# A twelfth ring slot for expert pieces, filled during the second mixer

## The chip, the cores and the metric

The kernel runs on one core of a Trainium2 chip. The metric is the device time of one execution in microseconds (us). The kernel before took 689.34 us, the median of three runs (689.18 to 690.75).

## The reference

One call computes two transformer blocks on 256 tokens of width 1024, all in float32.

- The first block is a mixer (a gated convolution and a gated linear attention in both directions) and a gated MLP of inner width 2816 with a convolution.
- The second block is a mixer (latent attention with 8 heads and an mLSTM with 4 heads, joined and multiplied by `w_o`), then a mixture of experts, then a gated embedding path ("PLE"), and a final norm.

The part that matters here is the mixture of experts and what follows:

```python
g_top, g_idx = lax.top_k(softmax(hf @ w_rg + b_rg), 1)               # 1 of 4 groups
e_top, e_idx = lax.top_k(softmax(e_in), TOP_K)                       # 2 of its 8 experts
# for each token and chosen expert e:
y = (silu(x @ w_g[e]) * (x @ w_u[e])) @ w_d[e]                       # 1024 -> 256 -> 1024
x = x + weighted sum of y
x = x + (p @ w_ple) * sigmoid(rmsnorm(x) @ w_ple_gate)
return rmsnorm(x, final_norm_g)
```

There are 32 experts with three matrices of 1024 x 256 each. Which experts a token takes is known only when the router has run, but with 256 tokens every expert's weights are loaded: 32 x 3 MB, about 100 MB of the 175 MB that the kernel moves.

## The kernel before

The program is written out by hand for each engine: a block of instructions for SP (SyncE, which issues nearly all loads), GpSimd, ScalarE, VectorE and TensorE. Each engine runs its own list in order, and semaphores tie the lists together. `sig(name)` is a semaphore; several steps that follow one another can share one (`STEPS`), and `at(name, n)` is the count at which step `name` has been done n times.

**Expert pieces.** The host lays the expert weights out as `w_moe`: 8 groups of 4 experts, each group cut into 6 pieces of 128 x 4096 floats (2048 KB): four for the gate and up matrices (a quarter of the 1024 rows each) and two for the down matrix. So there are 48 pieces. They come in through a ring of slots. Three more loads go through the same ring: `w_ple` (item 42, 1024 KB, put between pieces 41 and 42) and the two halves of `w_ple_gate` (the last two items, 49 and 50). An *item* is a place in that order of 51; up to item 41 item n is piece n, and items 43 to 48 are pieces 42 to 47.

**The ring.** The kernel before has 11 homes for items (`HOMES`, L339 to L343), each 4096 floats wide on all partitions: six slots of the tile `W` (which holds weight panels in the earlier stages), four stretches of the tile `arena` (work space of the earlier stages) and `hh` (the normed and the transposed tokens). Item n goes to home n mod 11. The homes come free at different times of the second mixer, so SP's list fills them one after the other as their last readers finish (L521 to L542): item 0 into `W` slot 2 once the query weights are used, parts of items 1, 2 and 4 piecemeal as attention gets on, item 3, then items 5 to 10. The last of these, item 10, goes into `hh` when the router's logits are done. From item 11 on (L545 to L559) SP waits until the piece that was 11 items before it has been used in the last round of its group, and then issues the load.

**The expert stage.** TensorE goes through the 8 groups in order. A group takes one or more rounds of 32 token slots for each of its 4 experts; here there are 9 rounds in all, two of them in the second group. A round is: gather the tokens (L2302), multiply them with the four up pieces (L2318), scatter the results of the round before (L2324), turn the activations, and multiply with the two down pieces (L2378). Ahead of each piece TensorE waits for its landing (`landed_chunk`, L2290). Ahead of the last group stands `ple_product` (L2402), which multiplies by `w_ple`. Five filler matmuls (L2374) stand ahead of the wait for the last down piece. Behind the last group come the last scatter, the transposes, and the product with `w_ple_gate`, whose weights are split on ScalarE (L1014) and VectorE (L1730) into a rounded part and a rest (`wpg_high`, `wpg_low`), as are the tokens (`hpT`).

**The mixer's weights.** At the end of the first block SP issues two panels of `w_in_2` (L500, L501), the query and key/value weights (L502, L503) and three small ones (L504 to L506). Then it waits for the first projection (`a2_used`) and issues one half of `w_o` (L508); then for the z product (`zw_used`) and issues the other half (L510). ScalarE rounds `w_o` in pieces between its other work (L893).

Of the kernel before, what the change touches and what calls it, by code (L numbers as in the profile page):

```python
# [22 lines left out]
P = 128  # L23
# [3 lines left out]
KD = D // P  # L27
# [27 lines left out]
CPG = UPC + DNC  # L55
NCHUNK = NGRP8 * CPG
UNIT = 4096
SLOTS = 6
RING = SLOTS + 5
PLE_AT = 42  # L60
# [9 lines left out]
def build(nc, a, out):  # L70
    with ExitStack() as ctx:
# [10 lines left out]
                        ("mq_done", 2), ("sa_done", 6), ("mk_done", 2), ("mv_done", 2), ("nt_done", 1)),  # L82
            "pe_route": (("oT_done", 2), ("hmT_done", 2), ("pT_done", 1), ("y2_done", 2), ("logits_done", 2), ("rank_done", 1)),
            "act_mix1": (("lr_ready", 1), ("q_ready", 1), ("ln_ready", 1), ("k_ready", 1), ("v_ready", 2),
# [11 lines left out]
                         ("max_ready", 12), ("nmax_ready", 1), ("nm_ready", 1)),  # L96
            "dve_route": (("hmn_ready", 8), ("ym_ready", 2), ("gsub_ready", 1), ("sel_ready", 1), ("msub_ready", 1)),
        }
# [28 lines left out]
        W_at = -(-nc.sbuf_base // 32) * 32  # L127
        W = sb("W", [P, SLOTS * UNIT])
        junk_at = -(-nc.sbuf_base // 32) * 32
        junk = sb("junk", [P, D])  # L130
# [207 lines left out]

        HOMES = [W[:, s * UNIT:(s + 1) * UNIT] for s in (2, 3)]  # L339
        HOMES += [arena[:, FRONT + s * UNIT:FRONT + (s + 1) * UNIT] for s in range(3)]  # L340
# [5 lines left out]
        def ring(n):  # L346

            return HOMES[n % RING]

        def item(chunk):  # L350
# [8 lines left out]
        pw = v3(ring(PW_ITEM)[:, 0:2048], 2)  # L359
        sgate = v3(ring(PLE_AT + 2)[:, 0:2048], 2)  # L360
        assert ring(PLE_AT + 1) is HOMES[RING - 1]

# [45 lines left out]
        wpg = [ring(NCHUNK + 1 + h).rearrange("p (k n) -> p k n", k=KD) for h in range(2)]  # L408
        assert (NCHUNK + 1) % RING == 5 and (NCHUNK + 2) % RING == 6
# [32 lines left out]
        def _(sp):  # L442
# [62 lines left out]
            sp.dma_start(wm[:, 1], a["w_mk_2"][0].rearrange("h d e -> d h e")).then_inc(sig("wm_landed"), 16)  # L505
            sp.dma_start(wm[:, 2], a["w_mv_2"][0].rearrange("h d e -> d h e")).then_inc(sig("wm_landed"), 16)  # L506
            sp.wait_ge(sig("a2_used"), 1)
# [5 lines left out]
            def load_chunk(n):  # L513
                g, j = divmod(chunk_of(n), CPG)
                sp.dma_start(ring(n), w_moe[g, j]).then_inc(sig(f"ring{n % RING}_landed"), 16)

# [10 lines left out]
            load_part(4, 0, 1800)  # L527
            sp.wait_ge(sig("sel_built"), 8)
            load_part(1, 3008, UNIT)
            sp.wait_ge(sig("st_done"), 6)  # L530
            load_part(1, 1536, 3008)
            load_part(2, 0, 2048)
            sp.wait_ge(sig("num_done"), 4)
            load_part(4, 1800, UNIT)
            sp.wait_ge(sig("pv_done"), 4)
            load_part(2, 2048, 3088)
# [147 lines left out]
        def _(act):  # L684
# [323 lines left out]
            def round_gate(pieces):  # L1008

                for n in pieces:  # L1010
                    h, q = divmod(n, 4)
                    m = NCHUNK + 1 + h
                    act.wait_ge(sig(f"ring{m % RING}_landed"), 16 * (m // RING + 1))
                    act.copy(wpg_high[h][:, 2 * q:2 * q + 2, :], wpg[h][:, 2 * q:2 * q + 2, :]).then_inc(sig("dense_high"), 1)  # L1014
# [63 lines left out]
        def _(dve):  # L1078
# [621 lines left out]
            for g in range(NGRP8):  # L1700
                if g == NGRP8 - 1:
                    for q in range(4):
                        b, half = divmod(q, 2)
                        dve.wait_ge(sig("pw_done"), q + 1)
# [41 lines left out]
            lower_gate((6, 7))  # L1746
            dve.wait_ge(sig("pw_ready"), 4)
            dve.wait_ge(sig("xs_ready"), 4)
# [19 lines left out]
        def _(pe):  # L1768
# [622 lines left out]
            def ple_product(done):  # L2391

                pe.wait_ge(sig("pT_ready"), at("pT_ready", 1))
                landed_chunk(PLE_AT)
                pe.wait_ge(sig("sc_ready"), done + 1)
                pe.wait_ge(sig("xgb_ready"), done + 1)
                for q in range(4):
                    b, half = divmod(q, 2)
                    if q >= 2:
                        pe.wait_ge(sig("pw_ready"), q - 1)  # L2400
# [4 lines left out]
                pe.wait_ge(sig("pw_ready"), 4)  # L2405

# [79 lines left out]
```

## Time and profile before

| | |
|---|---|
| median of three runs | 689.34 us |
| lowest, highest | 689.18, 690.75 us |
| span of the profiled execution | 686.0 us |
| time of the profiled execution beside its span | not recorded apart; the three runs above lie 3.2 to 4.8 us over the span |
| TensorE matmul, weight load | 636.9 us, 481.4 us |
| VectorE, ScalarE, GpSimd | 379.4, 277.6, 56.3 us |
| bytes moved | 174.75 MB, mean 255 GB/s |

How to read the rows further down. A row of the timeline has the start and the length of a piece of work in us, its engine, its line in the kernel, the operation, what it writes and reads, how many instructions were merged (x16), and in brackets how long the engine had been idle before and what ended that. SPq is SP's queue: its rows are the issues of loads, not their duration; a long one means that SP was held while issuing. A row of the stretches has the busy time of each engine with its count of instructions, then the clock granted to TensorE (1.00 is full), the mean busy share of the 16 DMA engines, and what they moved in GB/s. A row of the chain has a start, a length, and what the chain passed through. A row of the page's DMA issues has the size of each and the median time from issue to landing.

### The profile page before, as it was taken

Reading aid. Unit: us, or ns where it says so; the run is one execution under the profiler, and the core shown is the slowest. Engines: PE = TensorE matmul, PEld = TensorE weight load, DVE = VectorE, ACT = ScalarE, POOL = GpSimd, SP = SyncE. Lnnn points to the kernel's source line nnn. Section 1 sums busy time; section 2 is a strip of 40 time slices with the busy share of each in tenths; the row PEclk is TensorE's granted clock in tenths of the full one; section 3 lists DMA queues with packets and bytes.
Section 4 is the critical chain, followed back from the end, with each engine's and each line's share of the span. In section 5 each row is a group of like instructions: output and inputs, shape, how many; then the busy total and the mean of one; then the engine's idle time right before and its main releaser. Section 6 shows DMA issues by size and latency. Waiting matters only on the chain.

```text
span 686.0 us, 11096 instructions
## 1 busy us (share of the span) xinstructions
PE 636.9 (93%) x4347; PEld 481.4 (70%) x4347; DVE 379.4 (55%) x666; ACT 277.6 (40%) x431; POOL 56.3 (8%) x81
## 2 busy tenths in 40 slices
PE   7999999999999999999999999999999866768895
PEld 4999997799999999996697788744444332324364
DVE  6686965668766677767768465542222220203195
ACT  6764373556555555545755721311111000000193
POOL 1000000400000000003084610000000000000010
PEclk9999999999999999999999999999999998989998
DMA  8944541757755555204903548999899999999931
GB/s 324 349 144 148 199 147 33 262 159 244 234 187 187 188 187 188 97 0 140 330 38 122 188 182 308 364 425 427 362 431 426 428 427 428 427 425 428 408 140 61
DMA packets 55209, 174.75 MB, mean 255 GB/s; under 512 B 4743, under 2 KB 29443, under 8 KB 48899
## 3 DMA queue, kind: packets, MB, share of 16 engines
q1 hardware_dynamic: 54496, 172.54, 65.9%
q10 hardware_dynamic: 674, 1.69, 0.7%
q8 instruction: 26, 0.43, 0.3%
q14 instruction: 13, 0.10, 0.0%
HBM read 173.17 MB, written 1.05 MB: 254 GB/s over the span
## 4 chain that ended last, share of the span: by engine, by line
PE 68%; DMA 19%; DVE 7%; ACT 3%; issue 2%; another core or an unknown queue 0%; POOLq 0%; POOL 0%; DVEq 0%; ACTq 0%
PE ps L1801 15%; PE ps L1803 15%; PE ps L1802 15%; DMA arena<-in_w_moe_dram 14%; PE ps L2318 5%; DMA W<-in_w_moe_dram 4%; PE ps L2302 2%; PE ps L2378 2%; PE ps L1998 2%; PE ps L2324 1%; PE ps L2425 1%; PE ps L2146 1%; DVE arena L1458 1%; PE ps L2097 1%; PE ps L2161 1%
## 5 line engine op out<-in xcount | busy, mean ns | idle before, releaser
L1801 PE MATMUL ps<-hT_high,w_up_parts 128*128 128x256 f32 x352 | 99.8, 283 | 0.0
L1803 PE MATMUL ps<-hT_high,w_up_parts 128*128 128x256 f32 x352 | 99.6, 283 | 0.0
L1802 PE MATMUL ps<-hT_low,w_up_parts 128*128 128x256 f32 x352 | 99.6, 283 | 0.0
L1801 PEld LDWEIGHTS ps<-hT_high,w_up_parts 128*128 128x128 f32 x352 | 67.5, 192 | 0.5
L1802 PEld LDWEIGHTS ps<-hT_low,w_up_parts 128*128 128x128 f32 x352 | 67.5, 192 | 0.4
L1803 PEld LDWEIGHTS ps<-hT_high,w_up_parts 128*128 128x128 f32 x352 | 67.5, 192 | 0.0
L1289 DVE TENSOR_TENSOR w_up_parts<-W,w_up_parts 128x1024 fp32r<-128x1024 f32 x44 | 52.8, 1227 | 25.5 <-ACT w_up_parts L818 25.5
L818 ACT CAST w_up_parts<-W 128x1024 fp32r<-128x1024 f32 x44 | 44.7, 1047 | 29.7 <-PE ps L1803 29.7
L988 ACT ACTIVATE sg<-ps 128x256 f32<-128x256 f32 x9 | 3.5, 384 | 122.3 <-PE ps L2318 122.3
L1801 PE MATMUL ps<-h_high,dense_high 128*128 128x256 f32 x160 | 45.7, 286 | 0.0
L2318 PE MATMUL ps<-W,junk 128*32 128x512 f32 x304 | 37.2, 618 | 9.0 <-DMA W<-in_w_moe_dram 9.0
L1802 PE MATMUL ps<-h_low,dense_high 128*128 128x256 f32 x160 | 45.3, 283 | 0.0
L1803 PE MATMUL ps<-h_high,dense_low 128*128 128x256 f32 x160 | 45.3, 283 | 0.0
L1314 DVE SCALAR_TENSOR_TENSOR arena<-ps,arena 128x255 f32<-128x255 f32 x80 | 33.1, 477 | 17.5 <-ACT arena L838 17.1
L2302 PEld LDWEIGHTS ps<-arena,x_tok 128*128 128x128 f32 x288 | 32.9, 192 | 11.2 <-issue 11.2
L1172 DVE TENSOR_TENSOR dense_low<-W,dense_high 128x1024 fp32r<-128x1024 f32 x32 | 37.2, 1221 | 1.9 <-ACT dense_high L755 1.9
L2302 PE MATMUL ps<-arena,x_tok 128*128 128x128 f32 x288 | 34.5, 278 | 3.2 <-DVE arena L1654 2.0
L755 ACT CAST dense_high<-W 128x1024 fp32r<-128x1024 f32 x32 | 31.3, 1045 | 11.9 <-PE ps L1803 10.0
L1660 DVE TENSOR_TENSOR slots_low<-ps,slots_high 128x512 fp32r<-128x512 f32 x20 | 12.9, 686 | 35.6 <-ACT slots_high L992 35.3
L1801 PE MATMUL ps<-w_down_high,uact_high 128*128 128x512 f32 x80 | 31.3, 392 | 0.5 <-DVE uact_low L1325 0.5
L1681 DVE SCALAR_TENSOR_TENSOR sg<-sg,stat,ps 128x256 f32<-128x256 f32 x9 | 4.3, 480 | 49.3 <-ACT sg L988 49.3
L1801 PEld LDWEIGHTS ps<-h_high,dense_high 128*128 128x128 f32 x160 | 30.7, 192 | 1.1 <-issue 1.1
(480 smaller groups left out, 1355.4 us busy)
## 6 DMA issues: line engine op xcount, KB each, us to landing
W<-in_w_moe_dram SPq DMA_DIRECT2D x24, 2048.0 KB, 22.8
arena<-in_w_moe_dram SPq DMA_DIRECT2D x17, 2048.0 KB, 29.9
W<-in_w_up_dram SPq DMA_DIRECT2D x22, 1024.0 KB, 8.8
W<-in_w_in_dram SPq DMA_DIRECT2D x8, 2048.0 KB, 10.8
W<-in_w_down_dram SPq DMA_DIRECT2D x11, 1024.0 KB, 5.0
hh<-in_w_moe_dram SPq DMA_DIRECT2D x4, 2048.0 KB, 30.2
W<-in_w_out_dram SPq DMA_DIRECT2D x2, 2048.0 KB, 9.0
W<-in_w_o_dram SPq DMA_DIRECT2D x2, 2048.0 KB, 8.3
```

The source lines that it names most:

```text
L755: act.copy(piece(panel_hl(n)[0], n, c), piece(panel(n), n, c)).then_inc(sig("dense_high"), 1)
L818: act.copy(w_up_hl[0][:, c], U[q][:, :, g, i * P:(i + 1) * P]).then_inc(sig("up_high"), 1)
L1172: dve.tensor_tensor(piece(panel_hl(n)[1], n, c), piece(panel(n), n, c), piece(panel_hl(n)[0], n, c).bitcast(F32), ALU.subtract).then_inc(s ...
L1289: dve.tensor_tensor(w_up_hl[1][:, c], U[q][:, :, g, i * P:(i + 1) * P], w_up_hl[0][:, c].bitcast(F32), ALU.subtract).then_inc(sig("up_low" ...
L1314: dve.scalar_tensor_tensor(o, s, w, o, ALU.mult, ALU.add).then_inc(sig("tap_done"), 1)
L1801: pe.matmul(o, lhs[0], rhs[0], start=first, stop=False, skip_group_check=True)
L1802: pe.matmul(o, lhs[0], rhs[1], start=False, stop=False, skip_group_check=True)
L1803: return pe.matmul(o, lhs[1], rhs[0], start=False, stop=last_k, skip_group_check=True)
L1998: last = pe.matmul(ps[:, 2 + b, 0:424], hT[:, k, b * P:(b + 1) * P], wA[:, k, :], start=(k == 0), stop=(k == KD - 1))
L2302: last = pe.matmul(ps[:, h, (k % 4) * P:(k % 4 + 1) * P], x_tok[:, b, k * P:(k + 1) * P], hot[:, b, :], start=(b == 0), stop=(b == 1))
L2318: last = pe.matmul(ps[CAP * c:CAP * c + CAP, 2, :], xg[:, k, CAP * c:CAP * c + CAP], up_chunk(CPG * g + j)[:, c, kk, :], start=(k == 0), s ...
L2378: last = pe.matmul(ps[CAP * c:CAP * c + CAP, bank, :], aT[:, f, CAP * c:CAP * c + CAP], down_chunk(CPG * g + UPC + f)[:, c, 512 * half:512 ...
```

## The change

There are twelve homes. The new one is a tile of its own, `spare` (128 x 4096 floats), placed behind `W`; the room comes from the reserve for dynamic transfers, which the program now sets to 256 bytes. `spare` is home 0, and the other homes keep their order, each one place further on. SP issues item 0 into it right behind the three small mixer weights, ahead of both halves of `w_o`; each of the waits in the mixer that used to guard item n now guards item n + 1. From item 12 on a reload waits for the piece 12 items before it.

With another count of homes the last items fall elsewhere: the halves of `w_ple_gate` land in `W` slots 2 and 3 (before: `W` slot 0 and the last stretch of the arena), `hpT` moves from `W` slot 3 to slot 1, and `pw` and `sgate` (results of the PLE path) keep to homes whose last piece has been used. The semaphores of `pw_done` and `pw_ready` are given up for places on shared ones, which makes room for that of the twelfth home. The instructions on the compute engines are otherwise the same.

```diff
-RING = SLOTS + 5
+RING = SLOTS + 6
@@ STEPS
             "pe_route": (("oT_done", 2), ("hmT_done", 2), ("pT_done", 1), ("y2_done", 2), ("logits_done", 2), ("rank_done", 1),
+                         ("pw_done", 4)),
-            "dve_route": (("hmn_ready", 8), ("ym_ready", 2), ("gsub_ready", 1), ("sel_ready", 1), ("msub_ready", 1)),
+            "dve_route": (("hmn_ready", 8), ("ym_ready", 2), ("gsub_ready", 1), ("sel_ready", 1), ("msub_ready", 1),
+                          ("pw_ready", 4)),
@@
         W = sb("W", [P, SLOTS * UNIT])
+        spare = sb("spare", [P, UNIT])
@@
-        HOMES = [W[:, s * UNIT:(s + 1) * UNIT] for s in (2, 3)]
+        HOMES = [spare[:]] + [W[:, s * UNIT:(s + 1) * UNIT] for s in (2, 3)]
@@
+        def landings(n):
+            return 16 * (n // RING + 1) + (0, 0, 32, 32, 0, 16, 0, 0, 0, 0, 0, 0)[n % RING]
@@
-        sgate = v3(ring(PLE_AT + 2)[:, 0:2048], 2)
+        sgate = v3(ring(PLE_AT - 1)[:, 0:2048], 2)
@@
-        hpT = [v3(rounded(f"hpT_{part}", W_at, 3 * UNIT + n * UNIT // 2, UNIT // 2), KD) for n, part in enumerate(("high", "low"))]
+        hpT = [v3(rounded(f"hpT_{part}", W_at, UNIT + n * UNIT // 2, UNIT // 2), KD) for n, part in enumerate(("high", "low"))]
@@ SP
             sp.dma_start(wm[:, 2], a["w_mv_2"][0].rearrange("h d e -> d h e")).then_inc(sig("wm_landed"), 16)
+            ...
+            load_chunk(0)
             sp.wait_ge(sig("a2_used"), 1)
             sp.dma_start(PAN[5], w_o[:, :, 512:1024]).then_inc(sig("wo1_landed"), 16)
             sp.wait_ge(sig("zw_used"), 1)
             sp.dma_start(PAN[4], w_o[:, :, 0:512]).then_inc(sig("wo0_landed"), 16)
@@
             sp.wait_ge(sig("uq_used"), 1)
-            load_chunk(0)
+            load_chunk(1)
             sp.wait_ge(sig("mv_done"), at("mv_done", 2))
-            load_part(1, 0, 1536)
-            load_part(2, 3088, UNIT)
+            load_part(2, 0, 1536)
+            load_part(3, 3088, UNIT)
             ...
             sp.wait_ge(sig("y1_high"), 5)
-            load_chunk(3)
+            load_chunk(4)
             for n, (name, count) in enumerate((("half_used", 1), ("ym_ready", at("ym_ready", 2)), ("wo_used", 1), ("wo_used", 1),
-                                               ("wo_used", 1), ("logits_done", at("logits_done", 2))), 5):
+                                               ("wo_used", 1), ("logits_done", at("logits_done", 2))), 6):
                 sp.wait_ge(sig(name), count)
                 load_chunk(n)
@@ TensorE
             def landed_chunk(n):
-                pe.wait_ge(sig(f"ring{n % RING}_landed"), 16 * (n // RING + 1) + (0, 32, 32, 0, 16, 0, 0, 0, 0, 0, 0)[n % RING])
+                pe.wait_ge(sig(f"ring{n % RING}_landed"), landings(n))
@@
-    nc = _bacc.Bacc("TRN2", target_bir_lowering=False, num_devices=1)
+    nc = _bacc.Bacc("TRN2", target_bir_lowering=False, num_devices=1, dynamic_dma_scratch_size=256)
```

## Rows read from the trace of the kernel before

**Rows 1.** Page, busy time and DMA queues.
```profile
PE 636.9 (93%) x4347; PEld 481.4 (70%) x4347; DVE 379.4 (55%) x666; ACT 277.6 (40%) x431; POOL 56.3 (8%) x81
...
q1 hardware_dynamic: 54496, 172.54, 65.9%
```

**Rows 2.** Stretches: busy us by engine, clock, DMA share, GB/s.
```profile
346.00:378.00 32.00, 31.30 (x205) 26.85 (x204) 24.34 (x39) 16.73 (x26) 22.48 (x10) 1.00 0.19 66
...
442.00:486.00 44.00, 42.31 (x324) 21.11 (x324) 17.64 (x57) 7.54 (x13) 0.00 (x0) 1.00 1.01 428
...
486.00:492.00 6.00, 6.00 (x55) 2.35 (x58) 1.71 (x4) 0.00 (x0) 0.00 (x0) 1.00 0.67 224
...
492.00:650.00 158.00, 129.71 (x927) 56.52 (x919) 34.21 (x67) 12.41 (x28) 0.00 (x0) 0.95 1.01 426
```

**Rows 3.** Chain of waits, expert stage: start, length, what.
```profile
546.08 49.73 DMA arena<-in_w_moe_dram
...
602.66 44.64 DMA arena<-in_w_moe_dram
```

**Rows 4.** TensorE's timeline, expert stage.
```profile
546.69 1.93 PE L2318 MATMUL ps<-W,junk 128*32 128x512 f32 x16 [1.99 <-DMA W<-in_w_moe_dram]
...
595.85 1.92 PE L2318 MATMUL ps<-arena,junk 128*32 128x512 f32 x16 [0.82 <-DMA arena<-in_w_moe_dram]
...
600.74 1.92 PE L2318 MATMUL ps<-W,junk 128*32 128x512 f32 x16 [2.60 <-DMA W<-in_w_moe_dram]
...
618.24 8.04 PE L2402 MATMUL ps<-W,arena 128*128 128x512 f32 x16 [0.34 <-DMA W<-in_w_ple_dram]
...
642.53 1.92 PE L2378 MATMUL ps<-arena,sg 128*32 128x512 f32 x16 [0.47 <-DMA arena<-in_w_moe_dram]
...
647.34 1.92 PE L2378 MATMUL ps<-arena,sg 128*32 128x512 f32 x16 [1.52 <-DMA arena<-in_w_moe_dram]
```

**Rows 5.** SP's queue, second mixer.
```profile
326.62 5.10 SPq L506 DMA_DIRECT2D W<-in_w_mv_dram  x1
...
337.39 0.37 SPq L508 DMA_DIRECT2D W<-in_w_o_dram  x1
...
378.74 0.34 SPq L515 DMA_DIRECT2D W<-in_w_moe_dram  x1
```

**Rows 6.** SP's queue, beginning of the expert stage.
```profile
436.97 1.28 SPq L515 DMA_DIRECT2D W<-in_w_moe_dram  x3
...
465.96 0.33 SPq L515 DMA_DIRECT2D W<-in_w_moe_dram  x1
...
488.90 0.33 SPq L515 DMA_DIRECT2D arena<-in_w_moe_dram  x1
```

**Rows 7.** Stretches in the second mixer.
```profile
337.00:338.00 1.00, 0.70 (x5) 0.46 (x4) 1.00 (x3) 0.26 (x1) 0.00 (x0) 1.00 0.10 27
...
342.00:344.00 2.00, 2.00 (x19) 2.00 (x19) 1.90 (x10) 1.97 (x3) 0.00 (x0) 1.00 1.04 396
```

**Rows 8.** Page, DMA issues by tile: count, size, us to landing.
```profile
W<-in_w_in_dram SPq DMA_DIRECT2D x8, 2048.0 KB, 10.8
...
W<-in_w_o_dram SPq DMA_DIRECT2D x2, 2048.0 KB, 8.3
```

**Rows 9.** ScalarE's timeline, second mixer.
```profile
351.73 1.99 ACT L893 CAST wo_high<-W 128x1024 fp32r<-128x1024 f32 x2
...
357.31 0.60 ACT L917 ACTIVATE arena<-ps 128x512 f32<-128x512 f32 x1 [2.29 <-PE ps L1803]
```

**Rows 10.** ScalarE's timeline, tail.
```profile
652.79 3.90 ACT L1014 CAST wpg_high<-W 128x1024 fp32r<-128x1024 f32 x4
```

**Rows 11.** TensorE's timeline, a piece behind a wait.
```profile
576.04 3.45 PE L2318 MATMUL ps<-W,junk 128*32 128x512 f32 x16 [2.37 <-DMA W<-in_w_moe_dram]
```

**Rows 12.** Stretches with the granted clock, the same place and the tail.
```profile
576.00:579.40 3.40, 3.36 (x16) 0.59 (x16) 0.00 (x0) 0.00 (x0) 0.00 (x0) 0.53 1.01 429
...
647.30:661.00 13.70, 12.11 (x54) 6.18 (x55) 10.01 (x13) 9.43 (x14) 0.00 (x0) 1.00 0.80 298
```

More of the change, by code:

```diff
@@ L82, in build @@
                         ("mq_done", 2), ("sa_done", 6), ("mk_done", 2), ("mv_done", 2), ("nt_done", 1)),
-            "pe_route": (("oT_done", 2), ("hmT_done", 2), ("pT_done", 1), ("y2_done", 2), ("logits_done", 2), ("rank_done", 1)),
+            "pe_route": (("oT_done", 2), ("hmT_done", 2), ("pT_done", 1), ("y2_done", 2), ("logits_done", 2), ("rank_done", 1),
+                         ("pw_done", 4)),
             "act_mix1": (("lr_ready", 1), ("q_ready", 1), ("ln_ready", 1), ("k_ready", 1), ("v_ready", 2),
@@ L359, in build @@
         pw = v3(ring(PW_ITEM)[:, 0:2048], 2)
-        sgate = v3(ring(PLE_AT + 2)[:, 0:2048], 2)
-        assert ring(PLE_AT + 1) is HOMES[RING - 1]
+        sgate = v3(ring(PLE_AT - 1)[:, 0:2048], 2)
+        assert ring(NCHUNK) is HOMES[0] and ring(NCHUNK - 1) is HOMES[RING - 1]
         def up_chunk(n):
@@ L408, in build @@
         wpg = [ring(NCHUNK + 1 + h).rearrange("p (k n) -> p k n", k=KD) for h in range(2)]
-        assert (NCHUNK + 1) % RING == 5 and (NCHUNK + 2) % RING == 6
+        assert (NCHUNK + 1) % RING == 1 and (NCHUNK + 2) % RING == 2
         wpg_low = [rounded("wpg_low0", arena_at, FRONT, UNIT), rounded("wpg_low1", arena_at, FRONT + 3 * UNIT, UNIT)]
@@ L506, in _, with load_chunk @@
             sp.dma_start(wm[:, 2], a["w_mv_2"][0].rearrange("h d e -> d h e")).then_inc(sig("wm_landed"), 16)
+            def load_chunk(n):
+                g, j = divmod(chunk_of(n), CPG)
+                sp.dma_start(ring(n), w_moe[g, j]).then_inc(sig(f"ring{n % RING}_landed"), 16)
+            load_chunk(0)
             sp.wait_ge(sig("a2_used"), 1)
@@ L510, in _ @@
             sp.dma_start(PAN[4], w_o[:, :, 0:512]).then_inc(sig("wo0_landed"), 16)
-            def load_chunk(n):
-                g, j = divmod(chunk_of(n), CPG)
-                sp.dma_start(ring(n), w_moe[g, j]).then_inc(sig(f"ring{n % RING}_landed"), 16)
             def load_part(n, lo, hi):
@@ L521, in _ @@
             sp.wait_ge(sig("uq_used"), 1)
-            load_chunk(0)
+            load_chunk(1)
             sp.wait_ge(sig("mv_done"), at("mv_done", 2))
-            load_part(1, 0, 1536)
-            load_part(2, 3088, UNIT)
+            load_part(2, 0, 1536)
+            load_part(3, 3088, UNIT)
             sp.wait_ge(sig("conv2_done"), at("conv2_done", 4))
-            load_part(4, 0, 1800)
+            load_part(5, 0, 1800)
             sp.wait_ge(sig("sel_built"), 8)
-            load_part(1, 3008, UNIT)
+            load_part(2, 3008, UNIT)
             sp.wait_ge(sig("st_done"), 6)
-            load_part(1, 1536, 3008)
-            load_part(2, 0, 2048)
+            load_part(2, 1536, 3008)
+            load_part(3, 0, 2048)
             sp.wait_ge(sig("num_done"), 4)
-            load_part(4, 1800, UNIT)
+            load_part(5, 1800, UNIT)
             sp.wait_ge(sig("pv_done"), 4)
-            load_part(2, 2048, 3088)
+            load_part(3, 2048, 3088)
             sp.wait_ge(sig("y1_high"), 5)
-            load_chunk(3)
+            load_chunk(4)
             for n, (name, count) in enumerate((("half_used", 1), ("ym_ready", at("ym_ready", 2)), ("wo_used", 1), ("wo_used", 1),
-                                               ("wo_used", 1), ("logits_done", at("logits_done", 2))), 5):
+                                               ("wo_used", 1), ("logits_done", at("logits_done", 2))), 6):
                 sp.wait_ge(sig(name), count)
@@ L1012, in round_gate @@
                     m = NCHUNK + 1 + h
-                    act.wait_ge(sig(f"ring{m % RING}_landed"), 16 * (m // RING + 1))
+                    act.wait_ge(sig(f"ring{m % RING}_landed"), landings(m))
                     act.copy(wpg_high[h][:, 2 * q:2 * q + 2, :], wpg[h][:, 2 * q:2 * q + 2, :]).then_inc(sig("dense_high"), 1)
@@ L1703, in _ @@
                         b, half = divmod(q, 2)
-                        dve.wait_ge(sig("pw_done"), q + 1)
+                        dve.wait_ge(sig("pw_done"), at("pw_done", q + 1))
                         dve.tensor_copy(pw[:, b, 512 * half:512 * half + 512], ps[:, q % 2, :]).then_inc(sig("pw_ready"), 1)
@@ L1746, in _ @@
             lower_gate((6, 7))
-            dve.wait_ge(sig("pw_ready"), 4)
+            dve.wait_ge(sig("pw_ready"), at("pw_ready", 4))
             dve.wait_ge(sig("xs_ready"), 4)
@@ L2399, in ple_product @@
                     if q >= 2:
-                        pe.wait_ge(sig("pw_ready"), q - 1)
+                        pe.wait_ge(sig("pw_ready"), at("pw_ready", q - 1))
                     for k in range(2):
@@ L2404, in ple_product @@
                     last.then_inc(sig("pw_done"), 1)
-                pe.wait_ge(sig("pw_ready"), 4)
+                pe.wait_ge(sig("pw_ready"), at("pw_ready", 4))
             begun = 0
```

## The prediction

> **What bounds the kernel now.** I read the busy shares first, then the busy time by stretches, then the chain that ended last, and last TensorE's and SP's own timelines around the places that matter. The busy shares [rows 1] mislead: TensorE looks like the bound with 93%, and the main DMA queue fills two thirds of the 16 engines. The stretches take them apart [rows 2]. From 442 to 650 us, nearly the whole expert stage, the DMA engines are busy 1.01 of the time at 426 to 428 GB/s, except from 486 to 492 us, where the share is 0.67. From 492 to 650 us TensorE is busy 129.7 of 158 us. In the second mixer, by contrast, the DMA engines have room: their share is 0.19 from 346 to 378 us.
>
> The chain says the same [rows 3]: from 546 to 647 us it is two long DMA steps of expert pieces (49.7 and 44.6 us, each from the issue of a piece to its landing, with others ahead of it in the queue) and a few us of matmuls between them. Behind 647.3 us comes a tail of TensorE, ScalarE and VectorE work. TensorE's timeline shows what one piece costs [rows 4]: it waits for the landings of pieces 37 and 38, at 595.85 and 600.74 us, which are 4.89 us apart, and at the end for those of pieces 46 and 47, at 642.53 and 647.34 us. Piece 47 is the last one, and what follows takes 686.0 - 647.3 = 38.7 us.
>
> So the end is the landing of the last expert piece plus 38.7 us, and that landing is set by how many bytes are still to come when the DMA engines begin to be full at about 442 us.
>
> **The change part by part.**
>
> *One piece leaves the full stretch.* Item 0 now goes into a slot of its own and is issued right behind the three small mixer weights, near 331.7 us instead of at 378.74 [rows 5]. Every other home keeps its trigger: the home that took item n behind a given wait now takes item n + 1 behind the same wait. A reload of item n waits for the release of item n - 12, and that is what item n - 1 waited for before. So at each trigger in the program the loads are exactly one item further on. The place to test this is the one where the queue runs dry for want of a free slot [rows 6]: four items are issued from 437 to 442 us and six more, the first group's releases, up to 465.96; the next issue is at 488.90, when the second round of the second group has used its first piece. Ten transfers of 4.9 us last until about 487 us, hence the share of 0.67. After the change the same number of transfers stands between the same triggers: the gap stays, no longer and no shorter, and behind it 33 items are left instead of 34. Removed: one transfer of 2048 KB, 2.097 MB. By the rates of the full stretch (428 and 426 GB/s) it is 4.90 to 4.92 us; by two landings 4.89. I take -4.9 us.
>
> A rule may be weighed here. The rows show 426 to 428 GB/s. The Trainium skill, page "DMA: Bandwidth & Descriptors", section "Bandwidth", says that for loads from HBM the HBM side binds, at about 358 GB/s for a core; by it a piece is worth 5.9 us and the sum would be 683.5 us. The trace disagrees with it in this kernel, and the sum goes by the trace.
>
> *Does TensorE follow by the whole 4.9 us?* It waits for a piece at 546.69, nearly 2 us, the first such wait [rows 4]; up to there it keeps its times. From there to 650 us it is idle mostly ahead of landings. Where it has less slack than 4.9 us, only the next wait shrinks: it is ready for piece 37 at 595.03, with the landing now at 591.0, so it gains 0.8 us there; it is ready for piece 38 at about 597.3 and finds it landed; piece 39 lands one distance later, at 600.7 in place of 605.6, and there it waits again, the whole 4.9 us earlier. From there on what matters hangs on a landing or on a chain that began with one. The narrowest such chain goes from the landing of w_ple (618.24) over its product and the last group's gather and up products to 642.06, 0.47 us before piece 46 lands; ahead of piece 47 there are another 1.52 us of waiting. I take the whole 4.9; the lower end, if this chain ran 2 to 2.5 us longer, is 4.4.
>
> *What is put in front of the output weights.* Item 0 stands in SP's queue ahead of the second half of w_o, whose issue waits for the first projection until 337.39 us [rows 5]. SP is free from 326.62 + 5.10 = 331.72 us, and the issue of item 0 costs between 0.34 us (L515 at 378.74, into an idle queue) and 5.10 us (L506, the longest issue near it); SP is back at 336.8 at the latest, before the wait ends. Cost in SP's queue: 0. In the DMA engines: the weights ahead have drained by about 337 us (27 GB/s from 337 to 338), [rows 7], then w_o's half takes 8.3 us from issue to landing, to 345.7 us [rows 8]. With 2.1 MB ahead of it at 396 GB/s, 5.3 us, it lands at 351.0 us at the latest, and at 349 if item 0 begins at 336 already. Its first reader is ScalarE at 351.73 us [rows 9], and behind this reader ScalarE has another 2.29 us of idle, until TensorE's z product lets it go on. GpSimd takes the rounded half later still. Cost 0; upper end, if the landing slipped by the length of one more transfer to 356, 2 us.
>
> *The tail's homes.* The gate weights land in W slots 2 and 3 instead of W slot 0 and the arena. Their rounded copies go to W slots 4 and 5, which now hold up pieces of the last group, read before the down product at 642.53; the first rounding starts at 652.79 [rows 10]. hpT's halves go to W slot 1, an up piece of that group as well. hh holds the last group's first down piece, read until 644.45, and is written behind the last scatter. All these writes stand behind the last scatter by their own waits, so this cover doesn't depend on luck. Same number and shapes of instructions: 0, and no reason for a gain.
>
> *Semaphores and scratch.* pw_done and pw_ready move to shared counters whose earlier steps are complete by then; no wait is added: 0. The reserve for dynamic transfers goes from its default to 256 bytes. 172.54 of the kernel's 174.75 MB go over queue q1, named hardware_dynamic, issued by SP [rows 1]; GpSimd issues nothing. I take 0. No row bounds it from above but rival D; from below nothing can be gained.
>
> **Sum.** -4.9 us. The profiled span goes from 686.0 to 681.1 us. The profiled execution has no time of its own beside its span; the three runs lie 3.2 to 4.8 us above it and their median 3.3, which I keep: 689.34 - 4.9 = **684.4 us**. The runs' spread (689.18 to 690.75) puts it between 684.3 and 685.9, the lower end of the gain at 684.9.
>
> **Rivals.**
>
> *A. The clock takes part of it back.* Where TensorE has waited for a piece, its clock can fall: behind a wait of 2.37 us the 16 matmuls of a piece take 3.45 us, at a granted clock of 0.53, which is nearly all at the lower of its two levels (1.2 and 2.4 GHz); the same 16 take 1.92 us at 1.00 [rows 4, 11, 12]. None of this falls into the tail now: the granted clock is 1.00 from 647.3 to 661 us [rows 12]. With every wait moved, it could fall on the last down product, where nothing hides it: 1.5 us, so 685.9 us. Against it: the waits move together, their lengths hardly change, and the five filler matmuls still stand ahead of the last piece. The Trainium skill, page "TensorE: Matmul & The Clock Gate", section "Part 1: The HAM clock gate", tells that a pause in TensorE's activity brings the lower clock back; the rows agree, and it speaks against a change that makes TensorE wait more. Chance 0.08.
>
> *B. The room was not the limit.* If the ring is full by waiting for TensorE anyway, a piece loaded earlier only lengthens the gap at 486 to 492 us, or opens another: gain 0, 689.3 us. For it: the gap itself. Against it: a share of 0.67 in six us and of 1.01 everywhere behind. Chance 0.04.
>
> *C. w_o comes late: slower than before.* Item 0 holds up the second half of w_o, in SP's issue and in the queue. ScalarE's rounding at 351.73 stands in order ahead of the z gate and the mixer's conv activations. It costs from a landing after 351.73 + 2.29 = 354.0 us on, and outweighs the gain from 358.9. With the slowest reading of the rows (SP held once more by 5.1 us behind 337.4, then the 10.8 us from issue to landing that panels of w_in took [rows 8]) I get 353.3, still no cost. To be slower by 0.3%, over 691.4, it takes a landing at 361 us. Chance 0.03, about 692 us.
>
> *D. The smaller scratch slows the transfers.* 0.1 us on each of some 50 loads cancels the gain, 0.2 us on each gives 694 us. The queue's name speaks against it. Chance 0.03.
>
> **How the numbers follow.** Forecast 0.82 (684.4 us), A 0.08 (685.9), B 0.04 (689.3), C 0.03, D 0.03. A measurement of this kernel tells about 0.3%, 2.07 us, from no change, so faster means below 687.3 us: 0.82 + 0.08 = 0.90. Within 0.3%: 0.04 of B and 0.01 of C and D where they stay small, 0.05. Slower: the other 0.05 of C and D. The range holds the forecast's spread (to 685.9), 0.8 us below it for a faster set of runs or the page's rate, and A on top of a slower set: 683.6 to 687.0 us.
>
> **What would show it right or wrong.** Right: an issue of a 2048 KB expert piece near 332 us and full DMA engines until w_o's half has landed, before 351; ScalarE's reader still near 351.7; the first steps of the expert stage and the gap at 486 to 492 us at their present times; the waits for landings 4.9 us earlier by 600 us; the last down product at 642.4; a tail of 38.7 us. Wrong: that product at 642.4 but a longer tail (A); a longer gap (B); the expert stage beginning later (C); less than 426 GB/s in the full stretch (D).

## The result, and the profile after

The changed kernel took 683.26 us, the median of four runs (682.7 to 684.9), against 689.43 us of before (four runs, 689.18 to 690.75): ratio 0.9907 with a 95% interval of 0.9895 to 0.9920. Forecast were 684.4 us and a range from 683.6 to 687.0. The direction was right, and the time lies 1.1 us under the forecast and 0.3 us under the range. Three more comparisons, on three different chips (which chip the first one ran on is not on record), gave smaller gains:

| comparison | before | changed kernel | ratio | interval |
|---|---|---|---|---|
| first | 689.43 | 683.26 | 0.9907 | 0.9895 to 0.9920 |
| second | 690.10 | 685.45 | 0.9930 | 0.9917 to 0.9944 |
| third | 689.66 | 685.90 | 0.9944 | 0.9930 to 0.9957 |
| fourth | 689.97 | 684.91 | 0.9937 | 0.9914 to 0.9959 |

One run of before in the fourth comparison took 2198.93 us and is left out. The mean of the four ratios is 0.9930, a gain of 4.9 us. The intervals of the first and the third comparison do not meet (0.9920 and 0.9930): an interval from one set of runs does not cover what changes from one set to the next. So there are two things to explain: the 4.9 us, and why one comparison of a few runs can give 6.2 and another 3.8.

The span of the profiled execution after is 680.7 us. The stretches that answer to [rows 2 and 7] (busy us by engine, granted clock, DMA share, GB/s):

```profile
337.00:342.00 5.00, 5.00 (x43) 5.00 (x44) 3.85 (x9) 4.49 (x12) 0.00 (x0) 1.00 0.94 390
342.00:346.00 4.00, 4.00 (x36) 4.00 (x35) 1.82 (x11) 3.96 (x7) 1.01 (x1) 1.00 1.05 387
346.00:348.00 2.00, 2.00 (x19) 2.00 (x19) 0.00 (x0) 0.27 (x1) 1.92 (x2) 1.00 0.33 120
...
442.00:486.00 44.00, 42.31 (x328) 21.35 (x326) 17.62 (x56) 7.54 (x13) 0.00 (x0) 1.00 1.00 427
486.00:492.00 6.00, 6.00 (x57) 1.87 (x59) 1.45 (x3) 0.00 (x0) 0.00 (x0) 1.00 0.65 229
492.00:645.00 153.00, 130.02 (x924) 58.26 (x913) 34.54 (x67) 12.73 (x28) 0.00 (x0) 0.94 1.01 425
```

The reader is to see three things. From 337 to 346 us the DMA engines are now busy (0.94 and 1.05; they were at 0.10 from 337 to 338, [rows 7]) and the queue is empty at about 347. The gap at 486 to 492 us is where it was and as large, 0.65 against 0.67 [rows 2]. And the full stretch behind it, cut 5 us earlier at 645 us, still has a share of 1.01, at 425 GB/s: by share and rate it moved 153 us x 425 = 65.0 MB where before moved 158 us x 426 = 67.3 MB, about one transfer of 2.1 MB less.

SP's queue, with the new issue (L517 at 330.95), answers to [rows 5 and 6]; the last line is the first store of the output:

```profile
325.60 5.31 SPq L513 DMA_DIRECT2D W<-in_w_mv_dram  x1
330.95 0.51 SPq L517 DMA_DIRECT2D spare<-in_w_moe_dram  x1
336.68 0.37 SPq L521 DMA_DIRECT2D W<-in_w_o_dram  x1
...
436.22 1.28 SPq L517 DMA_DIRECT2D W<-in_w_moe_dram  x3
...
459.19 6.36 SPq L517 DMA_DIRECT2D arena<-in_w_moe_dram  x3
488.16 0.33 SPq L517 DMA_DIRECT2D W<-in_w_moe_dram  x1
...
672.20 6.17 SPq L573 DMA_DIRECT2D out_dram<-hh  x4
```

SP was held for 0.51 us by the new issue, and issued w_o's half at 336.68 as soon as its wait ended. The whole second block begins 0.71 us earlier than before (first panel at 317.31, was 318.02), and so does all of this: w_o's reader on ScalarE starts at 351.03 us (was 351.73, [rows 9]), the three loads at 436.22 (was 436.97), the first release of the second group at 488.16 (was 488.90). From the block's first panel to the three loads it is 118.91 us, and was 118.95. So the piece ahead of w_o cost the mixer nothing.

TensorE's timeline in the expert stage, with the waits for landings ([rows 4]):

```profile
590.52 1.92 PE L2326 MATMUL ps<-W,junk 128*32 128x512 f32 x16 [0.86 <-DMA W<-in_w_moe_dram]
...
595.42 3.33 PE L2326 MATMUL ps<-W,junk 128*32 128x512 f32 x16 [2.61 <-DMA W<-in_w_moe_dram]
...
600.32 1.92 PE L2326 MATMUL ps<-arena,junk 128*32 128x512 f32 x16 [1.56 <-DMA arena<-in_w_moe_dram]
...
612.94 7.11 PE L2410 MATMUL ps<-W,arena 128*128 128x512 f32 x16 [0.88 <-DMA W<-in_w_ple_dram]
...
637.38 1.92 PE L2386 MATMUL ps<-hh,sg 128*32 128x512 f32 x16
...
642.01 1.92 PE L2386 MATMUL ps<-spare,sg 128*32 128x512 f32 x16 [1.35 <-DMA spare<-in_w_moe_dram]
```

One row of before that stands nowhere yet is that of piece 39:

```profile
605.64 2.88 PE L2318 MATMUL ps<-arena,junk 128*32 128x512 f32 x16 [2.97 <-DMA arena<-in_w_moe_dram]
```

Piece 39 lands at 600.32 (was 605.64) and piece 47 at 642.01 (was 647.34): 5.32 and 5.33 us earlier, of which 0.75 were there before the three loads at 436.22 were issued. Behind piece 47 there are 680.7 - 642.0 = 38.7 us, the same tail as before. One more row of the chain shows the same bound as [rows 3]:

```profile
597.91 44.06 DMA spare<-in_w_moe_dram
```

### The profile page after: what moved, and what is told of

It reads as the page before. It is cut to its first block, busy times and chain, and to the rows that moved or that the text cites. A ratio compares the mean times of both kernels' runs of the same rounds, so it can differ in the third digit from the quotient of the medians.

```text
span 680.7 us, 11095 instructions
## 1 busy us (share of the span) xinstructions
PE 637.0 (94%) x4347; PEld 482.7 (71%) x4347; DVE 379.1 (56%) x666; ACT 277.7 (41%) x431; POOL 56.1 (8%) x81
## 3 DMA queue, kind: packets, MB, share of 16 engines
HBM read 173.17 MB, written 1.05 MB: 256 GB/s over the span
## 4 chain that ended last, share of the span: by engine, by line
PE 73%; DMA 14%; DVE 7%; ACT 2%; issue 2%; another core or an unknown queue 0%; POOL 0%; POOLq 0%; DVEq 0%; ACTq 0%
PE ps L1809 15%; PE ps L1811 15%; PE ps L1810 15%; DMA W<-in_w_moe_dram 7%; DMA spare<-in_w_moe_dram 6%; PE ps L2326 6%; PE ps L2310 3%; PE ps L2386 3%; PE ps L2332 2%; PE ps L2006 2%; PE ps L1781 1%; PE ps L2433 1%; PE ps L2154 1%; DVE arena L1466 1%; PE ps L2105 1%
## 5 line engine op out<-in xcount | busy, mean ns | idle before, releaser
L2326 PE MATMUL ps<-W,junk 128*32 128x512 f32 x368 | 46.2, 630 | 7.5 <-DMA W<-in_w_moe_dram 7.5
L2310 PEld LDWEIGHTS ps<-arena,x_tok 128*128 128x128 f32 x288 | 35.1, 203 | 11.2 <-issue 11.2
L2310 PE MATMUL ps<-arena,x_tok 128*128 128x128 f32 x288 | 36.7, 289 | 3.2 <-DVE arena L1662 2.0
L2326 PEld LDWEIGHTS ps<-W,junk 128*32 128x32 f32 x368 | 10.8, 113 | 31.1 <-issue 20.9
L1810 PE MATMUL ps<-w_down_low,uact_high 128*128 128x512 f32 x80 | 31.3, 391 | 0.0
```

What stands on the lines that cost most here:

```text
L1810: pe.matmul(o, lhs[0], rhs[1], start=False, stop=False, skip_group_check=True)
L2310: last = pe.matmul(ps[:, h, (k % 4) * P:(k % 4 + 1) * P], x_tok[:, b, k * P:(k + 1) * P], hot[:, b, :], start=(b == 0), stop=(b == 1))
L2326: last = pe.matmul(ps[CAP * c:CAP * c + CAP, 2, :], xg[:, k, CAP * c:CAP * c + CAP], up_chunk(CPG * g + j)[:, c, kk, :], start=(k == 0), s ...
```

## The experiments

Two measures serve below. The first is the time of the runs. The second is taken from each profile: from the issue of the three loads at the start of the full stretch (near 437 us) to the first store of the output. It leaves out all that happens in the first block and the mixer. I call it the expert span:

| kernel | expert span, us |
|---|---|
| before | 677.53 - 436.97 = 240.56 |
| reserve alone; tile alone | 240.62; 240.70 |
| changed kernel, four profiles | 235.98, 235.77, 235.68, 235.80 |

By it the ring of twelve gives 240.63 - 235.81 = 4.8 us, and no two profiles of one kind are more than 0.3 us apart. For the pair of profiles shown above it is 240.56 - 235.98 = 4.6 us.

**The reserve alone.** The kernel before with one edit:

```diff
-    nc = _bacc.Bacc("TRN2", target_bir_lowering=False, num_devices=1)
+    nc = _bacc.Bacc("TRN2", target_bir_lowering=False, num_devices=1, dynamic_dma_scratch_size=256)
```

> The kernel before with one edit: the reserve for dynamic transfers is 256 bytes; ring of eleven, all else as before. The changed kernel was 6.2 us faster by the medians where one transfer is worth 4.9; its four runs lie 1.9 to 2.1 us above their spans, where the profiled span of before (686.0) lies 3.2 to 4.8 us below the runs of before. Theory S (the smaller reserve shortens what lies around the span): time 688.0 to 688.4, that is 1.1 to 1.4 us below before, with time minus span near 2.0 here and near 3.3 in before. Rival N (what lies around the span doesn't depend on the reserve, and the extra 1.3 us are the luck of the runs): 689.0 to 689.9, time minus span the same as in the runs of before. Rival D of the prediction (a smaller reserve slows the transfers): slower than before, and less than 426 GB/s in the full stretch.

Measured: 689.98 us against 690.10, ratio 0.9997 (0.9988 to 1.0006), expert span 240.62 us. Theory S fell, and with it rival D of the prediction. Its reason fell too: time minus span is 1.8 to 2.1 us in all runs of this kernel and 1.7 to 2.1 us in those of before beside it. My "3.3 us above the span" had set the span of one run against the median of others.

**The room alone.** The tile is allocated and not used, so all behind `W` stands 16 KB further on; reserve 256 bytes.

```diff
         W = sb("W", [P, SLOTS * UNIT])
+        spare = sb("spare", [P, UNIT])
```

> The kernel before with the tile of the twelfth slot allocated behind W and never used (so junk, gbc, the constants and the arena stand 16 KB further on, as in the changed kernel) and the reserve at 256 bytes; ring of eleven. Theory T: addresses cost and give nothing, ratio 0.999 to 1.001, about the time of before. Rival X by addresses: up to 1.3 us faster, 0.998.

Measured: 689.94 us against 689.66, ratio 1.0000 (0.9991 to 1.0009), expert span 240.70 us. Addresses give nothing beyond the interval, 0.6 us either way.

**Item 0 late.** The changed kernel, with this:

```diff
-            load_chunk(0)
             sp.wait_ge(sig("a2_used"), 1)
...
                 sp.wait_ge(sig(name), count)
+                if n == 8:
+                    load_chunk(0)
                 load_chunk(n)
```

> The changed kernel with item 0 issued not ahead of w_o but between items 7 and 8, at the first wait that lets three loads go (near 436 us); twelve slots as in the changed kernel. Theory F (a transfer is worth its 4.9 us only if it is made while the DMA engines have room; from 437 us on they are full): the item stands in the full stretch again, so the gain over before is only what it fills of the gap at 486 to 492 us (a share of 0.67 in 6 us, 2.0 us): 2.0 us for the ring, plus whatever the reserve gives, so 2.6 to 3.3 us slower than the changed kernel, about 686.2, and the gap gone from the stretches. Rival R (twelve slots are worth it wherever item 0 is issued): like the changed kernel, 683.3. Rival B of the prediction would have the gap as long as before.

Measured: 687.20 us, ratio 0.9961 (0.9947 to 0.9975), against 685.45 us of the changed kernel in the same set. Stretches and queue:

```profile
486.00:492.00 6.00, 6.00 (x57) 2.18 (x60) 1.48 (x4) 0.00 (x0) 0.00 (x0) 1.00 0.99 423
492.00:648.00 156.00, 129.34 (x927) 57.25 (x919) 34.15 (x66) 12.27 (x28) 0.00 (x0) 0.95 1.01 425
```

```profile
436.83 0.33 SPq L517 DMA_DIRECT2D spare<-in_w_moe_dram  x1
437.20 1.46 SPq L517 DMA_DIRECT2D W<-in_w_moe_dram  x3
...
488.68 0.33 SPq L517 DMA_DIRECT2D W<-in_w_moe_dram  x1
```

The gap is gone: a share of 0.99 where it was 0.67, with eleven transfers instead of ten between the same triggers. The expert span, 675.67 - 436.83 = 238.84 us, is 1.8 us shorter than before's, close to the 2.0 us of idle in the gap, and 3.0 us longer than the changed kernel's. By the medians it is 1.75 us slower than the changed kernel (the intervals, to 0.9944 and from 0.9947, just fail to meet), less than the 2.6 to 3.3 expected; by the expert span the 3.0 us are as expected. So a twelfth slot is worth 1.8 us if it is filled when the DMA engines are full already, and 4.8 us if it is filled while they have room. Rivals R and B fell.

**Item 0 with item 1.**

```diff
-            load_chunk(0)
             sp.wait_ge(sig("a2_used"), 1)
...
             sp.wait_ge(sig("uq_used"), 1)
+            load_chunk(0)
             load_chunk(1)
```

> The changed kernel with item 0 issued right ahead of item 1, behind both halves of w_o (near 378 us in place of 331). The DMA engines have room there too: a share of 0.25 from 375 to 380 us and 0.10 from 385 to 390. Theory F: the same as the changed kernel within 0.5 us, since any place with room will do and item 0 ahead of w_o costs nothing. Rival W (item 0 ahead of w_o delays the mixer a little): faster than the changed kernel by up to 1 us. Rival L (items 2 and 3, issued from 389 us, come later for it and so on up to the full stretch): slower by up to 1 us.

Measured: 685.31 us, ratio 0.9934 (0.9920 to 0.9947), beside 685.45 of the changed kernel; expert span 673.01 - 437.01 = 236.00. Of the two places in the mixer neither is better: the expert spans are within 0.3 us, and the times say the same as far as their intervals go (about 0.9 us either way). Rivals W and L fell. But in its profile the mixer was 1.3 us longer (from 316.83 to 437.01, 120.2 us; 118.9 in the changed kernel). I first took that for a cost of the load; TensorE's rows say otherwise. Here is the same product in this kernel, and then in the changed kernel:

```profile
362.39 1.97 PE L2052 MATMUL ps<-arena 4*128 4x256 f32 x8
364.29 8.86 PE L2064 MATMUL ps<-arena,W 128*128 128x256 f32 x32
```

```profile
362.87 1.97 PE L2052 MATMUL ps<-arena 4*128 4x256 f32 x8
364.77 7.17 PE L2064 MATMUL ps<-arena,W 128*128 128x256 f32 x32
```

and the stretch from 366 to 369 us with the granted clock, in the same order:

```profile
366.00:369.00 3.00, 3.00 (x9) 2.39 (x8) 2.81 (x8) 0.56 (x2) 0.00 (x0) 0.54 1.04 396
```

```profile
366.00:369.00 3.00, 3.00 (x16) 2.65 (x15) 2.79 (x8) 0.80 (x2) 0.00 (x0) 1.00 1.04 399
```

The same 32 matmuls take 8.86 us and 7.17 us, and the granted clock is 0.54 against 1.00. The changed kernel itself showed 0.86 from 360 to 372 us in its third and fourth profile, and mixers of 120.1 us in both. Nor can item 0 be the cause here: in this kernel it is issued only at 378.78 us, behind that product.

**The changed kernel again**, three times, on the same chips as the other experiments.

> The changed kernel itself, on the same chip and in the same rounds as the other three. By the first comparison its ratio to before is 0.9907 (0.9895 to 0.9920), 5.5 to 7.2 us less. By one transfer alone (4.9 us) it would be 0.9929; by one transfer and 1.3 us around the span 0.9910. If the extra was luck the ratio goes to 0.993; if it is the reserve it stays near 0.991.

> The changed kernel a third time. So far 6.2 us less than before in the first comparison (0.9907) and 4.7 us in the second (0.9930, 0.9917 to 0.9944). Theory T (one transfer, 4.6 to 4.9 us; the first comparison was off by where short stretches of low clock fell in its runs): 0.9925 to 0.9935. Rival X (there is another lasting gain of over 1 us): 0.991 or less.

> The changed kernel a fourth time. Its gain over before was 6.2, 4.7 and 3.8 us. From the issue of the first three loads of the full stretch to the first store of the output the profiles agree far better: 240.6, 240.6 and 240.7 us for a ring of eleven, 235.7 to 236.0 us for the changed ring, 4.8 us less. Theory T: 4.8 us less than before, ratio 0.9930 within 0.0013, and 235.7 to 236.0 us in the profile. A ratio near 0.991 would speak for a gain that the first comparison saw and the profiles don't.

Measured: the rows of the table at the top. The second and fourth agree with theory T. The third, 0.9944, lies above what I expected (3.8 us), and the first lies below; the later three show that the extra was no lasting gain.

**One transfer less, without a slot.** The kernel before, with its ring of eleven. It leaves out all but 16 of the 4096 columns of item 30, so it computes with old data there, at the same shapes:

```diff
+                elif n == 30:
+                    g, j = divmod(n, CPG)
+                    sp.dma_start(ring(n)[:, 0:16], w_moe[g, j][:, 0:16]).then_inc(sig(f"ring{n % RING}_landed"), 16)
```

> The kernel before, but of item 30 (group 4's first piece behind two others, in the middle of the full stretch) only 16 of 4096 columns are loaded, so that part of the computation runs on old data; ring of eleven, all waits as before. It takes one transfer out of the full stretch without a twelfth slot. Theory T: the price of one transfer, 4.6 to 4.9 us less than before (0.9930), and the same as the changed kernel within 0.5 us. If TensorE's chain or the clock took a part back, less than 4; if the changed kernel had another gain beside the transfer, this one stays over 1 us slower than it.

Measured: 684.57 us, ratio 0.9925 (0.9911 to 0.9939), 5.1 us less; expert span 672.18 - 436.30 = 235.88 us, 4.75 less, and within 0.1 us of the changed kernel's. In the expert stage the price of one transfer accounts for the whole change. By the medians it is 1.3 us faster than the changed kernel beside it (685.90), where 0.5 us at most was expected; the intervals overlap. In the profiles the difference lies in the mixer: 118.93 us here, at full clock at 366 us, and 120.13 us in the changed kernel's third profile, at 0.50 there.

**Two and four transfers less**, in the changed kernel, by the same edit (items 30 and 34; items 26, 30, 34 and 38).

> The changed kernel, but of items 30 and 34 only 16 of 4096 columns are loaded, so parts of two groups are computed with old data. It asks what the next two transfers out of the full stretch would be worth. Theory T (the landing of the last piece sets the end, 4.8 us for each transfer): 9.6 us less than the changed kernel, about 675.5, ratio to before 0.979. Rival P (TensorE's own chain of 9 rounds is close behind): less than 4.8 us for the second one, 678 or more.

> The same with items 26, 30, 34 and 38. TensorE waits for landings 19 us in all in the changed kernel (from 540 to 645 us), so four transfers of 4.9 us are about as much as there is to gain. Theory T without a limit: 19.2 us less than the changed kernel, 665.8. Rival P: TensorE's chain becomes the bound; 12 to 17 us less, 668 to 673, with hardly any wait for a landing left and DMA engines that are idle in places behind 500 us. I think P the likelier here.

Measured: 675.01 us (0.9788, 0.9772 to 0.9804) and 665.25 us (0.9648, 0.9632 to 0.9664), beside before alone (689.56). The expert spans are 664.07 - 438.05 = 226.02 and 653.09 - 436.65 = 216.44 us: 9.8 and 19.4 us under the changed kernel's, 4.9 for each transfer, the fourth like the first. P, which I held the likelier for four, fell. The stretch of the kernel with four less:

```profile
492.00:622.00 130.00, 121.08 (x907) 56.63 (x899) 34.16 (x66) 11.75 (x26) 0.00 (x0) 0.99 1.01 426
```

The DMA engines are still full (1.01) and TensorE is busy 121.1 of 130 us, at a granted clock of 0.99. In the changed kernel, from 492 to 641 us (an end as far ahead of the last piece), it is busy 127.8 of 149 us, at 0.94. I had counted TensorE's busy time as fixed. Of the 19 us between the two stretches, 12.2 came out of waits for landings (18.7 us in the changed kernel, 6.5 here) and 6.8 out of the busy time. The up products show the same: from a piece in `W` a matmul takes 644 ns on average in the changed kernel and 596 ns here. Less waiting went with a higher clock, and the same matmuls took less.

**A filler in the first block's pause**, in the changed kernel, twice:

```diff
-            for k in range(24):
+            for k in range(32):
                 pe.matmul(ps[:, 3, 0:P], y1[0][:, k % KD, 0:P], y1[0][:, k % KD, 0:P], start=True, stop=True, skip_group_check=True)
```

> The changed kernel with 8 more filler matmuls (32 for 24, of 128x128) in the first block, between the transposes of the two token halves, where TensorE waits 1.12 us for VectorE. In the profiles of before, of the reserve alone and of item 0 late, the granted clock there is 0.72 to 0.85 from 123 to 131 us and the second block's first load is issued at 318.0; in three others it is 1.00 there and the load is at 316.8 to 317.3. Theory K (which of the two a run gets is set by this pause): always 1.00, load issued by 317.3, and runs that lie closer together and by 0.3 to 0.8 us lower than the changed kernel's. Rival: the filler changes nothing, or costs its own length where the wait is gone, up to 0.5 us.

> The changed kernel with the 8 more filler matmuls again, beside the changed kernel in the same rounds. The first time it was 684.79 us against 685.90 of the changed kernel (ratios to before 0.9935 and 0.9944, intervals overlapping). Its second block began at 316.54 us, earlier than any other's, but the profile had the low clock at 366 to 369 us. Theory K (the pause in the first block sets part of the spread): granted clock 1.00 from 123 to 131 us again, second block from 316.5 to 317.3, ratio to the changed kernel 0.9985 to 0.9995. Rival: no difference, 1.000.

Measured: 684.79 us (0.9935, 0.9922 to 0.9949) beside 685.90 of the changed kernel, and 684.58 us (0.9927, 0.9914 to 0.9941) beside 684.91. Both times a little lower (1.1 and 0.3 us), both times inside the intervals. The runs lie no closer together the first time (682.96 to 686.56, against 683.54 to 686.28); the second time they do (682.87 to 685.50), but only for one run of the changed kernel at 689.24. Its profiles have the clock at 1.00 from 123 to 131 us, but so has the changed kernel in every profile. It is unclear whether it gives anything.

## Why the prediction was right, and where it was wrong

The mechanism was right and so was the size of its gain, 4.9 us. What failed is the spread that was put around the sum.

**One piece leaves the full stretch: right.** 4.9 us were forecast. The changed kernel's expert span is 4.8 us shorter, the kernel with one transfer less gives 4.75, and the four comparisons give 4.9 in the mean. The gap stayed as it was (0.65 for 0.67), as reckoned from the triggers; the late issue shows that it is a matter of these triggers, since one transfer more between them closes it.

**TensorE follows: right.** The last waits moved by the same 5.3 us as the first ones behind 595 us, and the tail is unchanged at 38.7 us. Rival A did not happen on this path: the last down product took 1.92 us, at full clock. The walk through the single waits was wrong on the way, without a consequence for the end: it had TensorE gain only 0.8 us ahead of piece 37 and find piece 38 landed. In fact TensorE waited for both, at 590.52 and 595.42 us, 5.3 us earlier than before in each case, so it had followed by the whole amount already there.

**w_o: right, cost 0.** The DMA queue was empty by about 347 us, about 348 in the times of before, a little ahead of my 349 to 351; its reader did not move against the block's start (33.7 us behind it in both).

**Tail's homes, semaphores, scratch: right, 0.** The reserve alone is 0.9997, the room alone 1.0000, and the tail is as long as before. Rival D fell. The semaphores were not tried alone.

**The step that failed** is the spread around the sum: "The runs' spread (689.18 to 690.75) puts it between 684.3 and 685.9", and in the range "0.8 us below it for a faster set of runs". The term of 0.8 us was too small.

- The gain of the same change measured 6.2, 4.7, 3.8 and 5.1 us in four comparisons, with a mean of 4.9. The first lies 1.3 us above the mean, where the range left 0.8.
- The spread of one kernel is wider than three runs show. Over the runs of the second comparison before took 687.98 to 690.91 us, and the changed kernel 682.33 to 685.75.

A second sentence of the sum was wrong in itself but did no harm: "the three runs lie 3.2 to 4.8 us above it and their median 3.3, which I keep". What lies around the span is 2.0 us in every run (1.7 to 2.1, in before and after alike), so the profiled span of 686.0 belonged to a run of about 688 us, and the other 1.3 us were this run's distance from the median of others. In the second comparison the same could be read off: the run of before with a span of 686.1 took 687.98 us. The 3.3 us cancel in 689.34 - 4.9, so they moved neither the forecast nor its range.

The distance itself does not look like chance. In each of the 13 sets of runs whose profiled run is marked on record it is the fastest; in the changed kernel's four it lies 0.6, 3.3, 2.4 and 2.1 us below the median of the rest. So a profile describes a run that is faster than the typical one, and why is open. It explains little of the first comparison: without its profiled run the changed kernel's median there is 683.29.

Part of the spread between profiles can be named. It is the granted clock, in two places outside the expert stage. The first is at 123 to 131 us in the first block; before and then the changed kernel:

```profile
123.00:131.00 8.00, 6.88 (x36) 4.51 (x35) 6.52 (x11) 4.93 (x9) 6.29 (x27) 0.79 1.04 399
```

```profile
123.00:131.00 8.00, 6.88 (x50) 5.41 (x50) 6.42 (x11) 5.84 (x11) 5.77 (x25) 1.00 1.02 423
```

and SP's issues on both sides of it, first of before and then of the changed kernel:

```profile
118.28 0.88 SPq L462 DMA_DIRECT2D W<-in_w_down_dram  x2
...
151.73 0.37 SPq L462 DMA_DIRECT2D W<-in_w_down_dram  x1
```

```profile
119.20 0.88 SPq L469 DMA_DIRECT2D W<-in_w_down_dram  x2
...
150.97 0.37 SPq L469 DMA_DIRECT2D W<-in_w_down_dram  x1
```

From the one issue to the other it is 33.45 us at a clock of 0.79 and 31.77 us at 1.00: 1.7 us for a stretch of 8 us. This made up the 0.7 us by which the whole second block began earlier in the profile after (the changed kernel had been 0.9 us late until then). That it is not the change's doing is shown from both sides: the unused tile alone has 1.00 there, and the kernel with item 0 late, whose first block is the changed kernel's, has 0.79. The second place is the product at 364 us, 1.2 to 1.3 us of the mixer. Each of the two was at the low clock in some profiles and at full clock in others, of the same program in the second case.

One thing about the second place stays open. It was at full clock in all four profiles of kernels with eleven homes, and at the low clock in seven of the ten with twelve, the two runs with fewer transfers and the two with the filler among them. Item 0's load is not what does it, as the kernel with item 0 beside item 1 shows, but whether the change makes the low clock likelier there in another way, which would cost it about 1.2 us in such runs, no run settles.

In the first comparison three unprofiled runs of the changed kernel gave 683.2, 683.3 and 684.9 us; in the later ones thirteen gave 683.86 to 686.28, but for one of them at 689.24 with a mean clock of 0.932. So the extra 1.3 us belongs to that set of runs, or to its chip, and not to the kernel. That it comes from low stretches which those runs missed is likely and not shown. Their mean granted clocks were 0.985, 0.985 and 0.983, and eleven of the thirteen later ones had 0.982 or less; but the other two, at 0.984 and 0.986, took 685.34 and 685.92 us all the same. The chip is the other candidate: the later comparisons ran on three different chips, one each, so chip and set can't be told apart.

I had the size of such a stretch in the prediction (1.5 us, rival A) and used it only upward. Profiles with eleven and with twelve homes show it at the first place, so it belonged on both sides of the forecast: 684.4 with up to 2 us each way, 682.4 to 686.4. This is said with the results known; all four medians (683.26 to 685.90) lie in it.

## What to carry to other kernels

Where loads fill the DMA engines for a whole stage, ask what still goes through them when they begin to be full: in this kernel a slot was worth its transfer (4.8 us for 2 MB) when it was filled before that point, and only the idle time of the ring's gap (1.8 us) when it was filled after it. To check that nothing is given back later, pair each load with the wait that triggers it: if every trigger is one load further on, gaps stay as they are. For differences under 1% compare a span inside the profile that leaves out the places where the clock comes and goes; here such a span repeats within 0.3 us, where the whole spans of the same profiles differ by up to 1.1 us and the runs of one kernel by 3 us. And do not take one comparison's interval for the whole uncertainty: repeat the comparison.

## What the runs showed of the hardware that was not expected

- TensorE's clock fell near 366 us in the kernel with item 0 beside item 1 (0.54 from 366 to 369 us), inside a product of 32 matmuls, with no pause ahead of them but one of 0.31 us; 8 matmuls from only 4 partitions (1.97 us) stood between that pause and the product. In the changed kernel the same rows stood before 1.00. So it is not only waiting for data that goes with the lower of the two levels. The Trainium skill, page "TensorE: Matmul & The Clock Gate", section "Part 1: The HAM clock gate", tells of an activity monitor that sets the clock by how busy TensorE has been. The rows don't contradict it, but since the same instructions ran at either clock, no run here shows what made the difference.
- Removing waits gave TensorE back part of its busy time: the mean granted clock of the expert stage rose from 0.94 to 0.99 when four transfers were taken out, and the busy time fell by 6.8 us. So a bound reckoned from the busy time at the lower clock came out too early.
- The load rate of the full stretch held at 425 to 427 GB/s through all of this. The page "DMA: Bandwidth & Descriptors" of the Trainium skill (section "Bandwidth") would have made one piece 5.9 us; measured were 4.75 and 4.8. The first comparison's 6.2 us alone (5.5 to 7.2 by its interval) would have pointed to 5.9.
